# The start of the input projection in a hybrid decoder block: conditioning sums by TensorE in single columns, and a projection that begins with half of the tokens

## The reference

```
mod = silu(c) @ w_ada + b_ada                 # c: 1 x 1024, w_ada: 1024 x 6144
sh1, sc1, g1, sh2, sc2, g2 = split(mod, 6)
h = rmsnorm(x, norm_pre_mix) * (1 + sc1) + sh1
proj = h @ w_in                               # 1024 x 3072, all tokens
pa, pb, pc = proj[:, :1536], proj[:, 1536:2560], proj[:, 2560:]
# then differential attention on pa, RWKV-7 on pb, a gated MLP over chunks on pc,
# an output projection, and a mixture of 64 experts (8 for each token)
```

## Time and profile before

| | |
|---|---|
| median of 3 runs | 2318.48 us (2313.07 to 2322.95) |
| the profiled execution, its own time | 2318.01 us |
| its span in the profile | 2316.3 us |
| TensorE busy | 1915.6 us (83% of the span) |
| first matmul of the projection | 78.83 us into the span |
| first evacuation of a unit | 86.20 us |

### The profile page before, as it was taken

The page is one execution under the profiler, slowest core; times in us unless marked ns, Lnnn a source line. Parts: engine busy times, 40 slices in busy tenths (PEclk is TensorE's granted clock), DMA queues, the critical chain, the costliest instruction groups (busy, mean ns, idle before and its releaser), DMA issues. The chain is left out here.

```text
span 2316.3 us, 31665 instructions
## 1 busy us (share of the span) xinstructions
PE 1915.6 (83%) x8701; PEld 1372.7 (59%) x8702; DVE 1328.5 (57%) x2415; ACT 1008.2 (44%) x1810; POOL 466.9 (20%) x336
## 2 busy tenths in 40 slices
PE   2799997773887957998619999999999999999990
PEld 2688875552777853444316666666666676666660
DVE  6476615874677732333415666666766766666673
ACT  3222214652443412222215556655655665556562
POOL 0000000003222100212421333322323332233230
PEclk9899999985989968999859999999999999999995
DMA  8056202003110026342236998989989999899956
GB/s 338 1 181 227 81 6 70 16 16 146 39 40 6 6 93 243 70 71 62 56 112 199 301 301 249 300 243 345 341 233 288 346 359 288 242 305 303 321 112 236
DMA packets 130205, 416.40 MB, mean 180 GB/s; under 512 B 18276, under 2 KB 30909, under 8 KB 127054
## 3 DMA queue, kind: packets, MB, share of 16 engines
q1 hardware_dynamic: 96270, 288.76, 35.4%
q0 software_dynamic: 32720, 122.64, 20.4%
q10 hardware_dynamic: 1152, 4.19, 0.4%
HBM read 337.85 MB, written 77.94 MB: 180 GB/s over the span
## 5 line engine op out<-in xcount | busy, mean ns | idle before, releaser
L2006 DVE TENSOR_TENSOR w_low<-w_experts,w_high 128x1024 fp32r<-128x1024 f32 x392 | 453.9, 1220 | 131.0 <-ACT w_high L1968 120.2
L1968 ACT CAST w_high<-w_experts 128x1024 fp32r x392 | 381.8, 1046 | 102.0 <-issue 100.9
L2082 PE MATMUL ps_y<-w_experts,actT 128*128 x768 | 355.1, 606 | 37.9 <-issue 27.4
L2059 PE MATMUL ps_h<-w_high,xT_high 128*128 128x512 f32 x776 | 315.7, 407 | 4.4 <-DVE xT_low L2012 4.4
L2059 PE MATMUL ps_h<-w_high,xT_low 128*128 128x512 f32 x776 | 307.4, 396 | 0.0
L2059 PE MATMUL ps_h<-w_low,xT_high 128*128 128x512 f32 x776 | 307.3, 396 | 0.0
L1949 POOL DMA_INDIRECT acc<-y_rows,scatter_idx x96 | 152.4, 1588 | 703.0 <-DVE idx L1999 350.2
L2082 PEld LDWEIGHTS ps_y<-w_experts,actT 128*128 128x128 f32 x768 | 140.8, 193 | 185.2 <-issue 185.1
L1990 ACT COPY y_rows<-ps_y 128x512 f32<-128x512 f32 x96 | 56.4, 587 | 284.5 <-PE ps_y L2082 284.5
L1932 POOL DMA_INDIRECT gathered<-h,idx x99 | 167.4, 1691 | 44.3 <-issue 29.6
L2059 PEld LDWEIGHTS ps_h<-w_high,xT_high 128*128 128x128 f32 x776 | 147.3, 190 | 36.8 <-issue 2.9
(11 more groups left out here) (414 smaller groups left out, 3221.0 us busy)
## 6 DMA issues: line engine op xcount, KB each, us to landing
w_experts<-in_exp_w SPq DMA_DIRECT2D x384, 512.0 KB
qT<-in_w_ada POOLq DMA_DIRECT2D x16, 1024.0 KB, 5.3
w_raw<-in_w_in SPq DMA_DIRECT2D x24, 512.0 KB, 7.8
w_ada<-in_w_ada SPq DMA_DIRECT2D x8, 1024.0 KB, 12.0
pb<-pb_tile SPq DMA_DIRECT2D x16, 256.0 KB, 2.4
pb_cur<-pb SPq DMA_DIRECT2D x8, 512.0 KB, 3.9
pb_prev<-pb SPq DMA_DIRECT2D x8, 512.0 KB, 5.2
w_out<-in_w_out SPq DMA_DIRECT2D x1, 4096.0 KB, 16.1
```

What stands on the lines that cost most here:

```text
L1968: act.copy(w13_s[par][0][:, which, k], w13[:, bass.ds(w, 1), which, k].squeeze(1)).then_inc(w_high, 1)
L2006: dve.tensor_tensor(w13_s[par][1][:, which, k], w13[:, bass.ds(w, 1), which, k].squeeze(1), w13_s[par][0][:, which, k], ALU.subtract).then ...
L2059: q = pe.matmul(ps_h[:].rearrange("p (a n) -> p a n", a=2), xT[a][:, k, :], w13_s[par][z][:, :, k, :], start=(k == 0 and m == 0), stop=(k ...
L2082: q = pe.matmul(ps_y[n][:], aT[:, k, :], w2[:, bass.ds(w, 1), k, n * BANK:(n + 1) * BANK].squeeze(1), start=(k == 0), stop=(k == FC - 1))
```

## The change

1. The eight `ada_add` steps of the first part, and their column sums, are gone. TensorE works on each raw piece of w_ada as it lands: 16 matmuls for each piece, with a 128x128 slice of the piece stationary and the column of cond moving, each into its own column of PSUM bank 7 (128 columns in all). VectorE adds the 8 pieces with one reduction.
2. The loads are ordered: x tiles 0 to 3, weight group 0, x tiles 4 to 7.
3. The transposes of the first half of the tokens stand before unit 0; those of the second half stand in the projection, four chunks ahead of unit 1 and four ahead of unit 3, and use banks 4 to 7. Unit 0 waits for the first half of hT only, unit 4 for all of it. The transposes for the gated MLP stand behind unit 4.
4. For odd chunks k, ScalarE also writes the unrounded h, into a quarter of `acc[0]` (`full`), and VectorE only subtracts; for even chunks VectorE does both, as before.

```diff
@@ project: names
+        ada_cols = mod[:, 0:2 * KC]
...
+        full = [acc[0][:, n * BANK:(n + 1) * BANK] for n in range(KC // 2)]
+        h_bank = lambda b, k: bank[4 + k % 4] if b else bank[k]
@@ sync
-            for t in range(NT):
-                sp.dma_start(x[t], io["x"][0][t * P:(t + 1) * P, :]).then_inc(x_in[t], 16)
...
+            load_x(range(4))
             load_group(0)
+            load_x(range(4, NT))
@@ gpsimd
-                    pool.wait_ge(ada_sum, KC + n - 1)
+                    pool.wait_ge(ada_sum, n - 1)
@@ scalar
                     if b == 0 and k == 0:
                         act.wait_ge(mod_ready, 1)
-                        act.wait_ge(ada_sum, KC)
-                    act.activation(hT[0][:, k, b * BANK:(b + 1) * BANK], bank[k][:], ACT.Identity, scale=scale[:, k:k + 1],
-                                   bias=shift[:, k:k + 1]).then_inc(hT_high, 1)
+                    at, col, add = h_bank(b, k), scale[:, k:k + 1], shift[:, k:k + 1]
+                    act.activation(hT[0][:, k, b * BANK:(b + 1) * BANK], at[:], ACT.Identity, scale=col, bias=add).then_inc(hT_high, 1)
+                    if k % 2:
+                        if b:
+                            act.wait_ge(hT_low, k + 1)
+                        act.activation(full[k // 2], at[:], ACT.Identity, scale=col, bias=add).then_inc(full_ready, 1)
@@ vector
-            for k in range(KC):
-                dve.wait_ge(ada_in[k], 16)
-                ada_add(0, k, ada_first[k])
             dve.wait_ge(ada_mm, 1)
-            step.then(tt(shift[:], ps_s[:, 0:KC], cols[:, 0:KC], ALU.add))
-            step.then(tt(scale[:], ps_s[:, KC:2 * KC], cols[:, KC:2 * KC], ALU.add))
+            step.then(dve.tensor_reduce(ada_cols, ps_m[:, 0:2 * KC * KC].rearrange("p (k n) -> p n k", k=KC), AX.X, ALU.add))
+            step.then(tt(shift[:], ada_cols[:, 0:KC], cols[:, 0:KC], ALU.add))
+            step.then(tt(scale[:], ada_cols[:, KC:2 * KC], cols[:, KC:2 * KC], ALU.add))
...
-                    step.then(ts(zt[:], bank[k][:], scale[:, k:k + 1], shift[:, k:k + 1], ALU.mult, ALU.add))
-                    tt(hT[1][:, k, s], zt[:], hT[0][:, k, s], ALU.subtract).then_inc(hT_low, 1)
+                    if k % 2:
+                        dve.wait_ge(full_ready, b * (KC // 2) + k // 2 + 1)
+                        whole = full[k // 2]
+                    else:
+                        step.then(ts(zt[:], h_bank(b, k)[:], scale[:, k:k + 1], shift[:, k:k + 1], ALU.mult, ALU.add))
+                        whole = zt[:]
+                    tt(hT[1][:, k, s], whole, hT[0][:, k, s], ALU.subtract).then_inc(hT_low, 1)
@@ tensor
-            column_sums(0, ps_s, 0)
-            for b in range(2):
+            for k in range(KC):
+                pe.wait_ge(ada_in[k], 16)
+                if k == 0:
+                    pe.wait_ge(cond_ready, 1)
+                for n in range(2 * KC):
+                    q = mm(ps_m[:, 2 * KC * k + n:2 * KC * k + n + 1], ada_first[k][:, n * P:(n + 1) * P], cond[:, k:k + 1])
+            q.then_inc(ada_mm, 1)
+
+            def transpose_x(b, k):
                 pe.wait_ge(xn_ready, 4 * b + 4)
-                for k in range(KC):
-                    if b:
-                        pe.wait_ge(hT_low, k + 1)
-                    for t in range(4):
-                        q = pe.transpose(bank[k][:, t * P:(t + 1) * P], x[4 * b + t][:, k * P:(k + 1) * P], ident[:])
-                    q.then_inc(x_mm, 1)
-            pe.wait_ge(consts_in, 64)
-            pe.wait_ge(hT_low, 2 * KC)
-            for g in range(CG):
-                q = pe.transpose(ps_m[:, g * P:(g + 1) * P], w_s[:, g, :], ident[:])
-            q.then_inc(wsT_mm, 1)
+                if b == 0 and k == KC - 1:
+                    pe.wait_ge(mod_ready, 1)
+                if b:
+                    pe.wait_ge(hT_low, KC if k < 4 else KC + k - 3)
+                for t in range(4):
+                    q = pe.transpose(h_bank(b, k)[:, t * P:(t + 1) * P], x[4 * b + t][:, k * P:(k + 1) * P], ident[:])
+                q.then_inc(x_mm, 1)
+
+            for k in range(KC):
+                transpose_x(0, k)
...
+                if u in (1, 3):
+                    for k in range(2 * u - 2, 2 * u + 2):
+                        transpose_x(1, k)
+                if u == 0:
+                    pe.wait_ge(hT_low, KC)
+                if u == 4:
+                    pe.wait_ge(hT_low, 2 * KC)
...
+                if u == 4:
+                    pe.wait_ge(consts_in, 64)
+                    for c in range(CG):
+                        q = pe.transpose(ps_m[:, c * P:(c + 1) * P], w_s[:, c, :], ident[:])
+                    q.then_inc(wsT_mm, 1)
```

More of the change, by code:

```diff
@@ L118, in project @@
         act_step, dve_step = sem("act_step"), sem("dve_step")
+        cond_ready, full_ready = sem("cond_ready"), sem("h_full_ready")
         table_in, table_done, bias_mm, bias_rows_ready, bias_rows_out, bias_in = (sem(n) for n in (
@@ L132, in _, with load_x @@
                 sp.dma_start(ada_first[k], io["w_ada"][0][k * P:(k + 1) * P, 0:HALF]).then_inc(ada_in[k], 16)
-            for t in range(NT):
-                sp.dma_start(x[t], io["x"][0][t * P:(t + 1) * P, :]).then_inc(x_in[t], 16)
+            def load_x(tiles):
+                for t in tiles:
+                    sp.dma_start(x[t], io["x"][0][t * P:(t + 1) * P, :]).then_inc(x_in[t], 16)
             def load_group(g):
@@ L234, in evacuate @@
                     if g == Q and n == 0:
-                        act.wait_ge(ada_sum, 3 * KC)
+                        act.wait_ge(ada_sum, 2 * KC)
                     if g == K and n == 0:
@@ L272, in _ @@
             step.then(dve.reciprocal(e_col[:], e_col[:]))
-            step.then(tt(cond[:], c, e_col[:], ALU.mult))
+            tt(cond[:], c, e_col[:], ALU.mult).then_inc(cond_ready, 1)
             def ada_add(part, k, src):
@@ L281, in ada_add @@
                 q.then_inc(ada_sum, 1)
-                dve.wait_ge(ada_sum, part * KC + k + 1)
-            for k in range(KC):
-                dve.wait_ge(ada_in[k], 16)
-                ada_add(0, k, ada_first[k])
+                dve.wait_ge(ada_sum, (part - 1) * KC + k + 1)
             dve.wait_ge(ada_mm, 1)
-            step.then(tt(shift[:], ps_s[:, 0:KC], cols[:, 0:KC], ALU.add))
-            step.then(tt(scale[:], ps_s[:, KC:2 * KC], cols[:, KC:2 * KC], ALU.add))
+            step.then(dve.tensor_reduce(ada_cols, ps_m[:, 0:2 * KC * KC].rearrange("p (k n) -> p n k", k=KC), AX.X, ALU.add))
+            step.then(tt(shift[:], ada_cols[:, 0:KC], cols[:, 0:KC], ALU.add))
+            step.then(tt(scale[:], ada_cols[:, KC:2 * KC], cols[:, KC:2 * KC], ALU.add))
             stt(scale[:], scale[:], 1.0, cols[:, 48:56], ALU.add, ALU.mult).then_inc(mod_ready, 1)
@@ L396, in column_sums @@
             def column_sums(part, ps, at):
-                pe.wait_ge(ada_sum, (part + 1) * KC)
+                pe.wait_ge(ada_sum, part * KC)
                 for n in range(2 * KC):
```

## The result

The changed kernel takes 2331.36 us (median of 9 runs), the one before 2318.48 us (9 runs, 2313.07 to 2323.17). The ratio is 1.006, 95% interval 1.0032 to 1.0089: slower by 0.6%, some 13 us. 2331 was forecast. One of the nine runs of the changed kernel took 6874 us, for which nothing here shows a cause, and is left out of the ratio; the other eight took 2321.84 to 2346.81 us, with a median of 2330.5.

What follows compares the result with a forecast made beforehand. Bound: TensorE, busy 83% of the span; the change moves only the chain ahead of its dense stream. Sums +28.9, reduction +0.3, way to unit 8 -16.4: 12.7 us more, 2331 us, range 2323 to 2338.

Steps and rivals of the forecast that it cites:

- The price of a record: Conditioning sums on TensorE: 256 new records at 217.5 ns each, 55.7 us from 11.2 to 66.9, not 117 ns each.
- the reason given: Conditioning sums: they run at the lower clock level (1.2 GHz), and it is not the loads that slow them.
- I see nothing that would raise it: Clock during the sums: TensorE does nothing else until the last piece is summed, so the low clock stays.
- From the sums to the transposes: After the sums: 3.5 us as before plus 0.3 for the added reduction, so transposes start at 70.7.
- The way to unit 8: First transposes to the start of unit 8: shortens from 82.6 to 66.2 us.
- all of hT, ahead of unit 4: Second half of h: VectorE ends about 42.1 us behind the first transposes, hidden ahead of unit 4 by 1.3 us.
- last low piece of group 1: VectorE's low weights that unit 8 needs: done 66.2 us behind the first transposes.
- wait ahead of unit 8: TensorE waits for low weights, so unit 8 starts 0.6 us late.
- The clock didn't rise: Rival: the clock rises during the sums, which end at 41.2 to 43; 2306 us; chance 0.11.
- The stall in the woven part: Rival: interleaving stalls the stream at units 4 or 8, by up to 6 us, up to 2337; chance 0.09.
- That half of the tokens gives nothing: Rival: starting with half of the tokens brings no gain and the sums cost their full 29; 2347 us; chance under 0.01.
- its 16.4 us: Forecast gain on the way from the first transposes to unit 8, 82.6 to 66.2 us.

Runs made afterwards that it cites:

- Experiment 3: Changed kernel with 12 plus 28 unused transposes of the identity on TensorE before the first piece of w_ada is there; 2331.67 us (one run).
- experiments 4 to 6: Changed kernel with unused transposes among the sums: one before every second call, one before every call, two before every call; 2340.44, 2343.73 and 2368.61 us.
- experiment 10: Old conditioning, rest of the change, tiles scaled before the sums are awaited, plus unused transposes under the pieces and ahead of unit 0; 2304.94 us, ratio 0.9927.
- experiment 1: Changed kernel with the old conditioning (VectorE adds the pieces, TensorE sums 16 columns), all else as changed; 2302.23 us, ratio 0.9898 to the kernel before.
- experiment 7: Changed kernel with the old conditioning, and VectorE again makes the unrounded h of all chunks, without ScalarE's share; 2304.67 us, ratio 0.9935.
- experiment 8: Changed kernel with the old conditioning and the old load order, all eight tiles of x, then weight group 0; 2303.87 us, ratio 0.9929.
- experiment 6: Changed kernel with two unused transposes of the identity ahead of every call of the sums, 256 in all; 2368.61 us (one run).

## Why the prediction was right

**The price of a record** was the step on which the sign hung, and it held: 213.8 ns against 217.5, so the sums took 54.7 us, not 55.7. Experiment 3 shows that the reason given is the right one: it is the clock. "I see nothing that would raise it" was right, and understated: transposes among the sums don't raise it either (experiments 4 to 6). The Trainium skill's "TensorE: Matmul & The Clock Gate" (Part 1, "What's actually happening"), by which activity releases the throttle, disagrees with these runs for this form: 54.7 us of it without a gap released nothing. The Trainium skill's same page, Part 4 ("PE-mode transpose"), says that the full clock doesn't engage for transposes, which don't count as busy in the same way. It disagrees too: the 28 float32 transposes of experiment 3, behind 12 slow ones, took 3.25 us, the high rate. Here the measurements decide.

**From the sums to the transposes:** 0.29 us for the reduction against 0.3; 69.71 against 70.7, all of the difference from the sums.

**The way to unit 8,** behind the first transpose:

| | forecast | measured |
|---|---|---|
| last chunk of the first half | 11.2 | 11.2 |
| unit 0 starts | 16.0 | 16.0 |
| 16 transposes in the stream | 1.9 | 1.7 |
| all of hT, ahead of unit 4 | 42.1 | 41.7 |
| VectorE is free of `wsT_mm` | 49.4 | 49.0 |
| last low piece of group 1 | 66.2 | 65.5 |
| wait ahead of unit 8 | 0.6 | 0.2 |

The transposes' 1.7 us is the distance to the next matmul (92.70 to 94.37); their row's 1.91 overlaps with it. The rows that the prediction cites for 0.12 us each don't give that figure: they count records in half a microsecond, in which neighbours overlap. Unit 0 took 7.0 us, not 7.3. In the prediction's own terms the sums cost 27.9 us (28.9), the reduction 0.25 (0.3), and the way from the transposes to unit 8 shortened by 16.8 (16.4): 11.3 us at unit 8 where 12.7 were forecast. The median difference, 12.9, agrees with both within its interval, 7 to 21 us. That the median itself came out within half a microsecond of 2331 is luck: runs of the changed kernel lie up to 25 us apart, and between the two profiled executions the difference was 8.1 us.

**The rivals.** The clock didn't rise, and not by chance: in experiments 3 and 10 it even falls under one-column matmuls. The stall in the woven part was 0.2 us. That half of the tokens gives nothing was wrong by 16 us (experiment 1). The prediction didn't split its 16.4 us: experiment 7 gives ScalarE's share as 3.7 to 4.0 of them, of which the forecast path had 3.3 in the first half (11.2 against 14.5); the order of the loads gives none, as forecast (experiment 8).

## What to carry to other kernels

Before work moves onto an engine that "idles under the loads", compare the load's pace (2.5 us for each piece) with the price of the moved work at the rate which that engine will have there, here 6.8 us, not at the rate of the dense stream. Weight loads are busy for 54.69 of the 54.74 us, so I take them to be the price of a one-column matmul; no run varies them. VectorE keeps up with the 2.5 us of each piece and is the better place here. And take a change apart: its good part, alone, was worth 15.8 us up to unit 8, and a wait that it left in place (tiles scaled behind the sums) another 3.9.

## What the runs showed of the hardware

- One-column matmuls with a fresh 128x128 stationary operand, 256 records on end behind transposes at the high rate, let the granted clock fall from 1.00 to 0.50 near 14.4 us, 3.2 us after the first of them, and it stayed there for 49 us with TensorE busy all the time (experiment 3). The 32 records of experiment 10 show the fall too, 2.9 us after the first.
- Two 128-column transposes for every two such records, 95 us long, didn't lift it (experiment 6); transposes alone did (experiment 3: 12 in 2.79 us, then 28 in 3.25 us).
- A tile of x was ready about a microsecond later in each of the seven profiles in which TensorE works while the pieces of w_ada land (1/rms at 36.3 to 36.7 us) than in the five others (35.1 to 35.5). The cause is open.
- The granted clock shows 1.00 ahead of its first recorded change, also where TensorE runs at the lower level, so there only the count of records tells the rate. The same window of 2 us as in experiment 3, with 20 records there, shows 11 in the changed kernel:

```profile
12.00:14.00 2.00, 2.00 (x11) 1.00 1.03 434
```
